# The first product's fold moved forward, and the second weight sum made by VectorE instead of GpSimd

## The reference, cut to what matters

```
h = _rmsnorm(x, norm_mlp[l])
u = jax.nn.relu(jnp.einsum('bsd,df->bsf', h, w_up[l]))      # 2048 -> 8192
x = x + jnp.einsum('bsf,fd->bsd', u * u, w_down[l])         # 8192 -> 2048
```

## Time and profile before

| what | value |
|---|---|
| median of 3 runs | 973.25 us (970.35 to 974.61) |
| the profiled execution's own time | 970.65 us |
| its span | 968.9 us (1.75 us lie around it) |
| granted TensorE clock | 0.998 |
| TensorE matmul busy | 950.2 us, 98% |
| TensorE weight load busy | 815.6 us, 84% |
| VectorE busy | 782.1 us, 81% |
| ScalarE busy | 526.8 us, 54% |
| GpSimd busy | 116.3 us, 12% |

### The profile page before, as it was taken

The page is one execution under the profiler, slowest core; times in us unless marked ns, Lnnn a source line. Parts: engine busy times, 40 slices in busy tenths (PEclk is TensorE's granted clock), DMA queues, the critical chain, the costliest instruction groups (busy, mean ns, idle before and its releaser), DMA issues.

```text
span 968.9 us, 12019 instructions
## 1 busy us (share of the span) xinstructions
PE 950.2 (98%) x4920; PEld 815.6 (84%) x4920; DVE 782.1 (81%) x605; ACT 526.8 (54%) x420; POOL 116.3 (12%) x65
## 2 busy tenths in 40 slices
PE   8999999999999999999999999999999999999996
PEld 7888888888888878888888888888888888888885
DVE  6597768664555699899999989989998998998864
ACT  6754335344444566465665556556555655646642
POOL 0000000000000203203020220203212030230000
PEclk9999999999999999999999999999999999999999
DMA  9956452655547598898979889898998989878832
GB/s 341 401 186 249 159 203 93 239 202 189 175 174 247 184 295 245 288 263 265 317 253 293 238 290 278 274 322 238 301 246 274 296 268 315 239 240 225 307 119 88
DMA packets 35763, 237.85 MB, mean 245 GB/s; under 512 B 3968, under 2 KB 4224, under 8 KB 7808
## 3 DMA queue, kind: packets, MB, share of 16 engines
q1 hardware_dynamic: 29232, 190.85, 51.0%
q0 software_dynamic: 6192, 45.09, 23.9%
q10 hardware_dynamic: 288, 1.18, 0.3%
HBM read 235.01 MB, written 2.10 MB: 245 GB/s over the span
## 4 chain that ended last, share of the span: by engine, by line
PE 73%; DVE 11%; issue 11%; DMA 2%; ACT 2%; SPq 0%; ACTq 0%; DVEq 0%
PE ps L397 26%; PE ps L400 14%; PE ps L488 9%; PE ps L579 6%; PE ps L581 6%; PE ps L585 6%; PE ps L623 4%; DVE w_lo L1175 3%; DMA w_raw<-w_stream 2%; DVE x L1205 2%; DVE act_b L1194 1%; ACT w_hi L793 1%; DVE val L1189 1%; DVE val L1185 1%; DVE w_lo L1009 1%
## 5 line engine op out<-in xcount | busy, mean ns | idle before, releaser
L397 PE MATMUL ps<-act_a,w_hi 128*128 128x512 f32 x1472 | 349.7, 390 | 0.0
L1175 DVE TENSOR_TENSOR w_lo<-w_raw,w_hi 128x2048 fp32r<-128x2048 f32 x120 | 324.3, 2702 | 8.3 <-ACT w_hi L793 7.2
L397 PEld LDWEIGHTS ps<-act_a,w_hi 128*128 128x128 f32 x1472 | 274.1, 188 | 55.5
L793 ACT ACTIVATE w_hi<-w_raw 128x2048 fp32r<-128x2048 f32 x120 | 229.4, 1913 | 76.5 <-PE ps L585 53.3
L400 PEld LDWEIGHTS ps<-act_a,w_lo 128*128 128x128 f32 x1472 | 188.6, 191 | 7.0
L400 PE MATMUL ps<-act_a,w_lo 128*128 128x256 f32 x1472 | 191.1, 283 | 0.0
L914 DVE TENSOR_TENSOR w_lo<-w_raw,w_hi 128x2048 fp32r<-128x2048 f32 x52 | 118.5, 2290 | 67.1 <-ACT w_hi L656 66.4
L579 PE MATMUL ps<-w_hi,act_b 128*128 128x512 f32 x392 | 153.9, 393 | 7.3 <-DVE x L1205 7.3
L581 PE MATMUL ps<-w_hi,act_b 128*128 128x512 f32 x392 | 153.3, 391 | 0.0
L656 ACT ACTIVATE w_hi<-w_raw 128x2048 fp32r<-128x2048 f32 x52 | 99.0, 1912 | 63.8 <-PE ps L400 39.0
L1175 DVE TENSOR_TENSOR w_lo<-mix_mem,w_hi 128x2048 fp32r<-128x2048 f32 x42 | 96.2, 2291 | 40.3 <-ACT w_hi L793 39.8
(11 more groups left out here) (103 smaller groups left out, 589.0 us busy)
## 6 DMA issues: line engine op xcount, KB each, us to landing
w_raw<-w_stream SPq DMA_DIRECT2D x108, 1024.0 KB, 6.5
w_raw<-w_quads SPq DMA_DIRECT2D x50, 1024.0 KB, 8.8
mix_mem<-w_quads POOLq DMA_DIRECT2D x28, 1024.0 KB, 10.2
mix_mem<-w_quads SPq DMA_DIRECT2D x14, 1024.0 KB, 4.7
w_raw<-w_quads POOLq DMA_DIRECT2D x14, 1024.0 KB, 10.5
w_raw<-w_stream SPq DMA_DIRECT2D x16, 256.0 KB, 8.2
x<-x_rows SPq DMA_DIRECT2D x2, 1024.0 KB, 15.8
mix_mem<-x_t SPq DMA_DIRECT2D x3, 512.0 KB, 8.5
```

The lines of the kernel that those rows point to most:

```text
L397: return pe.matmul(ps[:, bank, :], weights_hi, act, start=first, stop=False)
L793: act.activation(w_hi[:, g % 4, :], raw, ACT.Copy).then_inc(hi_ready, 1)
L1175: dve.tensor_tensor(out=w_lo[:, g % 4, :], in0=raw, in1=w_hi[:, g % 4, :].bitcast(F32), op=ALU.subtract).then_inc(lo_ready, 1)
```

## The change

The diff, whole. In GpSimd's program the sum for t2 goes. In VectorE's it stands behind `add_up` and ahead of the lo of `a11_b11`. The fold of `a11_b11` moves to just behind the lo of `n6_t2`; the fold of step 0's own `s7_t3` moves from ahead of it to behind the lo of up 1.

```
@@ gpsimd
             make_t3(0)
             for d in range(SEVENS):
-                pool.wait_ge(lo_ready, ITEM["s7_t3", d] + 1)
-                pool.wait_ge(raw_loaded[2], 16 * (FIRST_UP + LEAD + d + 1))
-                pool.tensor_tensor(out=sums[d % 2], in0=sums[d % 2], in1=w_raw[:, 2, :], op=ALU.add)\
-                    .then_inc(t2_added, 1)
                 if d + 1 < SEVENS:
                     make_t3(d + 1)
-                pool.wait_ge(t2_added, d + 1)
                 pool.wait_ge(lo_ready, ITEM["a11_b11", d] + 1)
                 add_quad(w_raw[:, 2, :], d, 1, t1_added)
                 pool.wait_ge(lo_ready, ITEM["n6_t2", d] + 1)
@@ vector
                 add_up(t - 1)
+                dve.wait_ge(lo_ready, ITEM["s7_t3", d] + 1)
+                dve.wait_ge(raw_loaded[2], 16 * (FIRST_UP + LEAD + d + 1))
+                dve.tensor_tensor(out=sums[d % 2], in0=sums[d % 2], in1=w_raw[:, 2, :], op=ALU.add)\
+                   .then_inc(t2_added, 1)
                 lo_of(ITEM["a11_b11", d], w_raw[:, 2, :])
...
                 up_lo(t, 1)
                 if d:
                     fold("a22_t4", d - 1, bank_b(d - 1), 1, 0, ALU.add)
+                else:
+                    fold("s7_t3", 0, bank_b(0), 1, 1, ALU.subtract)
...
                 dve.wait_ge(t2_added, d + 1)
                 lo_of(ITEM["n6_t2", d], sums[d % 2])
+                fold("a11_b11", d, NT, 0, 0, ALU.add)
                 if folding:
                     quad_lo(s, A12, val[:, :, 0:P])
                 lo_of(ITEM["a12_b21", d], w_raw[:, 3, :])
-                if d == 0:
-                    fold("s7_t3", 0, bank_b(0), 1, 1, ALU.subtract)
-                fold("a11_b11", d, NT, 0, 0, ALU.add)
                 if folding:
```

## The result

| | kernel before | changed kernel |
|---|---|---|
| median of 6 runs | 972.83 us (970.35 to 974.87) | 963.27 us (962.45 to 965.78) |
| ratio | | 0.9906, 95% interval 0.9887 to 0.9925 |
| profiled execution, span | 968.9 us | 961.7 us |
| from up 0 of step 0 to the plain products | 587.42 us | 579.19 us |

The change makes the kernel faster, by 9.1 us going by the ratio (7.3 to 11.0); forecast were 8.2 us and a time of 964. The last row is from the weight loads' timelines (329.45 to 916.87 before, 330.50 to 909.69 after). It leaves out the kernel's front, the part ahead of step 0, which the change doesn't touch and which took 1.05 us longer in this one execution. It is the closest measure that the two traces give, and it says 8.23 us, inside the interval of the timed runs.

What follows compares the result with a forecast made beforehand. TensorE, busy for 98% of the span, was taken to bound the kernel, so only its gaps count. 6.97 + 1.24 = 8.2 us off 971.95 gave 963.7, rounded to 964 us; range 961 to 969.5 us.

Steps and rivals of the forecast that it cites:

- Only gaps of TensorE count, and there are seven: TensorE's weight loads idle seven times for a fold, six even steps and step 0; worth at most 9.1 us.
- Part 1: GpSimd's sum goes, no longer disturbing VectorE's lo of `n3_b22`; of 3.83 us, `add_up` starts 1.56 us earlier.
- Part 2: VectorE's added sum, behind `add_up`, takes 2.21 us; the lo of `a11_b11` starts 0.65 us later.
- The cover in front of `a11_b11`: Fold of `n3_b22` still ends before TensorE starts `a11_b11`; 0.62 us left, some 0.7 us more in odd steps.
- Part 3: Fold of `a11_b11` moves behind the lo of `n6_t2`; the 1.15 us stall goes whole in six even steps.
- Step 0: TensorE's 2.16 us wait for a fold in the first step: 1.24 us gained, 0.92 us stays.
- The adding DMAs: GpSimd's DMAs for t1 and t4, released 0.65 us later, take 8.0 to 13.4 us; neither lands late.
- the first rival: Something else holds `add_up`, so the cover before `a11_b11` is gone and TensorE stalls there; about 970.5 us, chance 0.08.
- The sum of 8.2 us: Total predicted gain: 6.97 us from the even steps' stalls plus 1.24 us from the first step.
- The middle of four runs, 971.95: Middle of 970.35, 970.65, 973.25 and 974.61 us for the kernel before, from which the gain was subtracted.

Runs made afterwards that it cites:

- e1_folds: Kernel before with only the two folds moved as in the change, GpSimd keeping the sum; 961.97 us, ratio to before 0.9886.
- e4_early: Changed kernel with VectorE's sum put ahead of `add_up` instead of behind it; 961.97 us, ratio to before 0.9888.
- e3_nosum: Kernel before with GpSimd's sum and the waits for it left out, nobody adding the quadrant, folds at old places; 963.8 us, ratio to before 0.9903.
- e2_sum: Changed kernel with both folds put back, so only the sum goes from GpSimd to VectorE; 980.38 us, ratio to before 1.0073.
- e5_twosums: Changed kernel with VectorE's sum made twice in a row, the second waiting for the first; 982.93 us, ratio to before 1.0107.
- e6_both: Changed kernel with GpSimd's sum back at its old place and VectorE's behind it; 974.12 us, ratio to before 1.0018.
- e8_rest: Kernel before with the fold of `a11_b11` moved in steps 1 to 13 and left in step 0; 965.04 us, ratio to before 0.9924.
- e7_step0: Kernel before with the folds moved in step 0 alone; 968.54 us, ratio to before 0.9963.

## Why the prediction was right

- *Only gaps of TensorE count, and there are seven*: right. All were gone in `e1_folds` and `e4_early`, for 9.20 us; 9.1 had been read from the rows.
- *Part 1, 1.56 us of 3.83 arrive*: right. VectorE waits 2.17 us for `cross` in the trace after, and `add_up` begins 3.99 us ahead of up 0 (577.97 to 581.96) where it began 2.39 us ahead: 1.60 us earlier, the same as in `e3_nosum`.
- *Part 2, the sum costs 2.21 us*: right. 2.284 us each, 2.21 from start to start (580.37 to 582.58). With part 1 it is a loss of 0.65 us a step on the path; `e2_sum` showed 0.62 in each even step. So the difference of the two engines' own durations for the sum was not to be had, as the prediction argued: the exchange alone makes the kernel slower.
- *The cover in front of `a11_b11`*: right, 0.63 against 0.62, and `e5_twosums` spent it.
- *Part 3, the fold*: right, 1.15 us in each of six steps, and the term that carries the gain (`e1_folds`).
- *Step 0*: 0.90 us of its wait stay, 0.92 forecast.
- *The adding DMAs*: they landed in 7.9 to 12.3 us (before 8.0 to 13.4), and TensorE waited for none of them.
- *Too small*: the first rival's price. It left out that VectorE carries its backlog over; made real, in `e6_both`, it was 974.12 us. Its 970.5 us is also off by its own sum: 0.8 us less than the 971.95 on which the forecast was put is 971.2. The sum of 8.2 us left out the clock and the front, and carried the gain of one execution near the fastest to the median unchanged.
- *Luck*: the mechanism and its terms came out, but part of the closeness of 964 to 963.27 us is chance. The middle of four runs, 971.95, was 0.88 us under the median of before in the result (972.83), and the 8.2 us were 1.4 us under the difference of the medians (9.56); the two offset each other, and each lies within the spread of the runs.

## What to carry to other kernels

When one engine is busy throughout, look for the few gaps in front of it and ask what stands in their releaser's way; here moving two folds gave the whole gain, and taking the sum from one engine and giving it to another gave none. A disturbance of 3.8 us is worth what arrives at the next common wait, not its length, and idle time ahead of such a wait is the place for added work. Work out how much cover is left at each gate behind the edit, and check that the engine still catches up within the step, or the cover is spent by the step before.

## What the runs showed of the hardware that was not expected

A pause of TensorE can cost more than its length. In `e2_sum` 4.03 us of idle time, behind fully busy work at the full clock, were followed by at least 4.8 us at a granted clock of 0.50; in `e8_rest` 2.16 us were followed by some 3.3 us at 0.50, and pauses of 2.39 to 2.48 us ahead of the MLP in `e1_folds`, `e7_step0` and `e6_both` by as much. The same 2.16 us in the profiled execution of before, 2.70 us in step 0 of `e5_twosums`, and 2.96 us ahead of the MLP in `e3_nosum` (ending at 48.06) had no such stretch behind them. The length of a pause alone did not decide it in these traces.
